# Gated linear attention: level and diagonal products as 32- and 64-wide squares, one to a column group of the array

## The reference, cut to what matters

```python
def _gla_chunkwise(q, k, v, lf, S):
    ...
        b = jnp.cumsum(lfc, axis=2)
        o = jnp.einsum('bhtk,bhkv->bhtv', qc * jnp.exp(b), S)
        pair = jnp.exp(jnp.where(tri, b[:, :, :, None, :] - b[:, :, None, :, :], -jnp.inf))
        a = jnp.einsum('bhtk,bhtsk->bhts', qc, pair * kc[:, :, None, :, :])
        o = o + jnp.einsum('bhts,bhsv->bhtv', a, vc)
```

## Time and profile before

| | |
|---|---|
| median of 3 runs | 4092.09 us (4091.87 to 4096.19) |
| the profiled execution's own time | 4100.84 us |
| its span | 4099.1 us |
| TensorE busy | 3935.4 us, 96% of the span |
| VectorE, ScalarE, GpSimd busy | 37%, 31%, 21% of the span |
| the attention stage that is changed | about 1590 to 2412 us of the span |

### The profile page before, as it was taken

How to read it: one execution, slowest core, us unless ns; L and a number is a source line. 1 busy time by engine, 2 the same in 40 slices (tenths; PEclk the granted TensorE clock), 3 DMA queues, 4 the chain that set the end, 5 groups by cost and what they waited for, 6 DMA issues and landing times.

```text
span 4099.1 us, 38980 instructions
## 1 busy us (share of the span) xinstructions
PE 3935.4 (96%) x15382; PEld 2318.2 (57%) x15382; DVE 1497.8 (37%) x2687; ACT 1257.4 (31%) x2313; POOL 862.4 (21%) x885
## 2 busy tenths in 40 slices
PE   7999999999999999999999999988999899999998
PEld 3555555655665546777777754435666644444443
DVE  2433332122221004777777731456666510010000
ACT  3444442222230023444444422764444300000000
POOL 0000000000100003666666630233434300000000
PEclk9999999999999999999999999999999999999999
DMA  5121012011002111100111021211001012222111
GB/s 203 44 88 44 29 30 89 1 62 62 1 31 103 57 61 62 38 34 35 40 42 42 27 75 51 77 63 42 20 38 39 24 46 80 90 77 73 65 71 49
DMA packets 23189, 225.74 MB, mean 55 GB/s; under 512 B 2528, under 2 KB 5088, under 8 KB 7520
## 3 DMA queue, kind: packets, MB, share of 16 engines
q1 hardware_dynamic: 23008, 223.25, 14.7%
HBM read 221.14 MB, written 2.10 MB: 54 GB/s over the span
## 4 chain that ended last, share of the span: by engine, by line
PE 91%; DVE 3%; ACT 2%; issue 2%; DMA 1%; POOL 1%; POOLq 0%; DVEq 0%; ACTq 0%; SPq 0%
PE bank L1088 8%; PE bank L1374 7%; PE bank L1035 6%; PE bank L1098 4%; PE bank L849 4%; PE bank L946 4%; PE bank L802 4%; PE bank L1385 4%; PE bank L1209 3%; PE bank L1007 3%; PE bank L1078 3%; PE bank L1350 3%; PE bank L788 3%; PE bank L1141 2%; PE bank L976 2%; PE bank L868 2%
## 5 line engine op out<-in xcount | busy, mean ns | idle before, releaser
L1088 PE MATMUL bank<-hT,ring 128*128 128x256 f32 (+1 forms) x1024 | 345.2, 486 | 0.0
L1374 PE MATMUL bank<-hT,ring 128*128 128x512 f32 x704 | 303.9, 595 | 2.4 <-DVE hT L1921 2.4
L1088 PEld LDWEIGHTS bank<-hT,ring 128*128 128x128 f32 x1024 | 189.9, 190 | 119.7 <-issue 108.1
L1035 PE MATMUL bank<-Y,ring 128*128 128x512 f32 (+1 forms) x704 | 249.2, 517 | 0.0
L1374 PEld LDWEIGHTS bank<-hT,ring 128*128 128x128 f32 x704 | 134.3, 191 | 172.0 <-issue 170.7
L1035 PEld LDWEIGHTS bank<-Y,ring 128*128 128x128 f32 x704 | 134.5, 191 | 114.7 <-issue 108.0
L1209 PE MATMUL bank<-hT,ring 128*128 128x512 f32 x384 | 181.7, 608 | 14.2 <-ACT arena L1758 8.8
L849 PE MATMUL bank<-hT,ring 128*128 128x256 f32 (+1 forms) x512 | 186.3, 500 | 2.4 <-ACT hT L1451 2.4
L802 PE MATMUL bank<-hT,ring 128*128 128x256 f32 (+1 forms) x512 | 182.3, 493 | 0.0
L1437 ACT ACTIVATE arena<-xT 128x512 f32<-128x512 f32 (+1 forms) x56 | 31.7, 568 | 484.3 <-PE bank L779 379.4
L1098 PE MATMUL bank<-ring,hT 128*128 128x128 f32 x1536 | 179.0, 275 | 0.0
(11 more groups left out here) (404 smaller groups left out, 6980.3 us busy)
## 6 DMA issues: line engine op xcount, KB each, us to landing
ring<-in_w SPq DMA_DIRECT2D x60, 2048.0 KB, 7.9
ring<-in_w SPq DMA_DIRECT2D x17, 1536.0 KB, 7.0
ring<-in_w SPq DMA_DIRECT2D x20, 1280.0 KB, 5.5
ring<-in_w SPq DMA_DIRECT2D x12, 1024.0 KB, 4.8
ring<-in_w SPq DMA_DIRECT2D x8, 1408.0 KB, 6.0
ring<-in_w SPq DMA_DIRECT2D x19, 512.0 KB, 3.6
xT<-in_xT SPq DMA_DIRECT2D x1, 3072.0 KB, 12.0
out<-arena SPq DMA_DIRECT2D x1, 2048.0 KB, 6.2
```

Source lines behind the costliest of these rows:

```text
L1035: ins = e.matmul(m[:, 0:b - a], w[:, k, sl(j % 2)], src[:, k, a:b], start=k == 0, stop=k == kt - 1)
L1088: ins = e.matmul(m[:, 0:b - a], w[:, k, sl(1 + d)], hT[:, k, a:b], start=k == 0, stop=k == 7)
L1374: ins = e.matmul(m, w[:, k, sl(2 * i + j % 2)], hT[:, k, 0:LAT], start=k == 0, stop=k == 7)
```

## The change

Each level's product, and the diagonal's, is computed only in the squares that can hold pairs of the level. `squares_of(m)` lists them. For m = 64 these are two squares of 64 x 64 in each chunk, the two off-diagonal ones. For every other level, and for the diagonal, they are four squares of 32 x 32: with m = 32 each key block of 32 against its neighbour's queries, below that each against its own. Each square is a matmul of its own, with 32 (or 64) stationary columns, 32 (or 64) moving columns and all 128 rows. It writes to the output partitions that its keys stand for, so that the four (two) squares of a chunk lie in four (two) different column groups of the array. What is left of the bank is not written; the masks let none of it through, and of the diagonal's bank it is written over later. The other engines' instructions stay as they are.

```diff
@@ -589,6 +589,16 @@
+        def squares_of(m):
+
+
+            n = 64 if m == 64 else 32
+            for c in range(NT):
+                for g in range(128 // n):
+                    r = g ^ 1 if m >= 32 else g
+                    yield (slice(128 * c + n * g, 128 * c + n * g + n), slice(128 * c + n * r, 128 * c + n * r + n),
+                           slice(n * g, n * g + n))
+
@@ -1128,8 +1138,8 @@
                 k = gl_QK[spot["gl_dqk", j]]
-                for c in range(NT):
-                    ins = e.matmul(m[:, sl(c)], k[:, sl(c)], gl_q_[j % 2][:, sl(c)], start=True, stop=True)
+                for kc, qc, p in squares_of(1):
+                    ins = e.matmul(m[p, qc], k[:, kc], gl_q_[j % 2][:, qc], start=True, stop=True)
                 ins.then_inc(up("gl_d_mm", j), 1)
@@ -1137,8 +1147,8 @@
                 x = gl_QK[spot["gl_qk", j, li]]
-                for c in range(NT):
-                    ins = e.matmul(m[:, sl(c)], x[:, 512 + 128 * c:640 + 128 * c], x[:, sl(c)], start=True, stop=True)
+                for kc, qc, p in squares_of(LEVELS[li]):
+                    ins = e.matmul(m[p, qc], x[:, 512:1024][:, kc], x[:, qc], start=True, stop=True)
                 ins.then_inc(up("gl_m_mm", (j, li)), 1)
```

## The result

| | before | changed |
|---|---|---|
| median of 4 runs each, side by side | 4093.44 us (4091.87 to 4096.19) | 4061.01 us (4059.42 to 4062.71) |
| ratio, 95% interval | | 0.992 (0.9903 to 0.9937) |
| profiled execution, its span | 4100.84, 4099.1 us | 4061.02, 4059.2 us |
| a head, from norm to norm | 52.24 us | 50.00 us |

The change makes the kernel faster by 0.8%: 32.4 us between the medians, 34 were forecast. Between the two profiled executions lie 39.8 us, but the one of before was slow for its kernel, 7.4 us above the median. The head tells more than either: it is 2.24 us shorter, and the forecast's sum of 36.0 us, shared among 16 heads, is 2.25 each. From the first head's diagonal to the first projection behind the last head the stage takes 814.82 us before (1599.00 to 2413.82) and 780.35 after (1598.04 to 2378.39): 34.5 us less.

A forecast was written before the change was run, and what follows sets the result against it. TensorE's unbroken row of matmuls bounds the kernel. 32-square groups save 34.7 us, 64-square groups 1.3, the last head gives back 1.6: net 34, so 4092.1 - 34 = 4058 us, range about 4047 to 4088.

The forecast's parts named there:

- the forecast's sum of 36.0 us: Saving over all heads: 34.7 us from 112 groups of 32-squares plus 1.3 us from 16 groups of 64-squares.
- The bound: In the stage's steady part TensorE's matmuls run unbroken, so a microsecond of matmul less is a microsecond of time less.
- A round, 0.030 us: Four 32-column records, one per column group, stream side by side in 30 ns; eight rounds make a group's 0.24 us.
- rival 1: Weights are not hidden inside a group of squares: 57 ns a round, about 9 us less, 4083 us; chance 0.11.
- The visit, 0.34 us: Cost of going from full-width matmuls into column groups and out: entry, first weights, emptying and exposed full-width weights, 0.34 us.
- The cover, 0.29 us a level: GpSimd needs 3.73 us a level, levels afterwards start 4.02 apart, so it keeps up by 0.29; waits cost nothing.
- rival 2: GpSimd or VectorE holds TensorE at four levels a head: 19 us given back, 4077 us; chance 0.10.
- The last head: TensorE waits for GpSimd before five of seven levels there, so 5 x 0.31 = 1.6 us are given back.
- Rivals 1 and 3: Rival 1 as above; the other: short squares don't overlap, 1.30 us a 32-square group, 4144 us, chance 0.11.
- Rival 4: Instructions between levels don't arrive fast enough, 56 ns each: 0.6 us more a level, 4169 us; chance 0.03.

The follow-up runs named there:

- e4: The changed kernel with the diagonal back in four full-width matmuls, only the levels in squares: 4068.39 us, ratio 0.993.
- e5: The kernel before, with one 32 x 32 square put ahead of each level's four full-width matmuls: 4141.87 us, ratio 1.011.
- e7: The kernel before, with four extra full-width matmuls of only 32 moving columns ahead of each level's four: 4192.33 us, ratio 1.0235.
- e6: The changed kernel with an extra set of squares, all into the first column group, ahead of each level's own: 4166.04 us, ratio 1.0166.
- e1: The changed kernel with its squares ordered by column group, all four chunks of one group before the next group: 4110.93 us, ratio 1.0037.
- e10: The changed kernel with squares ordered by column group two chunks at a time, four records of a group in a row: 4066.93 us, ratio 0.993.
- e11: The changed kernel with each level's whole set of squares computed twice, set after set, column groups alternating: 4101.47 us, ratio 1.0013.
- e8: The changed kernel with levels 32 and 16, 8 and 4, 2 and 1 paired, two levels in one visit: 4049.64 us, ratio 0.9886.

## Why the prediction was right

- **The bound.** TensorE's row of matmuls without a gap carried the gain one to one: 2.24 us a head less in the squares, 2.24 us a head less in the period. e4, e5 and e7 moved the head by 0.31, 2.62 and 6.25 us, as their groups' own changes add up.
- **A round, 0.030 us.** The rounds of four start 32 ns apart, not the 57 of rival 1. e6 has 31 ns a record within a group, and the change's eight rounds take 0.25 us where 0.24 stood. 64-squares: 0.61 us in the chain, 0.45 + 0.16 forecast.
- **The visit, 0.34 us.** From L761 and L916 (entry 0.09, first weights 0.03, emptying 0.11, full-width weights 0.11). The single starts of the change give 0.09, 0.02, 0.11 and 0.10, 0.33 in all. e5 measures 0.31 by itself, with a single square.
- **The cover, 0.29 us a level.** The forecast held, no wait in 735 us (rival 2), but this figure was not what covered it. 4.03 us is the distance of two levels only; in the same chain the last two of a head start 2.31 apart (1729.17 to 1731.48), less than GpSimd's 3.73. What counts is how long a product lies ready before its matmuls. By the trace of the second to the fourteenth head that is at least 1.41 us for GpSimd's before and 1.51 after, both at a head's first level, and 1.64 and 1.04 us for VectorE's, both at the fourth. The prediction allowed for 0.9 us of the first level's margin to go; it grew by 0.1, and the smallest one is now VectorE's.
- **The last head.** 1.6 us were to be given back, which leaves 0.65 of 2.25; it kept 0.86. Right in kind; the size came out near although the wait grew by 2.6 us, and what made up for it was not measured.
- **Rivals 1 and 3** were wrong for one reason: weights and squares of different column groups overlap. The Trainium skill (TensorE: Matmul & The Clock Gate, "The mechanism") has loads pulled ahead of running matmuls when their row group differs or when they go to a background weight buffer. Here all use all rows, and 32 loads take 0.35 us beside 32 matmuls, so the condition on the row group, on which rival 1 leaned, does not bind, as it did not in the earlier trace rows. Whether the buffer is the reason no run here shows.
- **Rival 4** was wrong where it was put: 56 ns an instruction was a rate that streaming set, and 32 pairs of load and matmul now start in 0.39 us. A trace of it may stand behind the 33rd record of a visit (0.05 us), which the change never reaches.

One premise of the text was too simple, at no cost here: it took the groups for streams that don't hold each other up. e1 and e6 show that this holds only while no more than three records wait for one group. The change lists the chunk outside and the group inside, which is the good order.

The stage's 34.5 us compares with the sum's 34.4 (36.0 less 1.6). The median's 32.4 us is uncertain by some 7 (its interval, 26 to 40 us). It does not contradict 34, and that the two lie so close says no more than that.

## What to carry to other kernels

A masked product that fills only small blocks can go to column groups if the array visits them seldom: price the visit first (0.3 us here, as much as three full-width 128-column records), put as many squares as possible into one visit, and write them so that neighbouring instructions go to different groups (with four records in a row to one group little was lost, with eight the whole gain). A visit's price shows partly on the neighbours' lines, so measure from a landmark of the stage (here norm to norm) and not by the changed line alone. Terms can be taken from another stage of the same trace if the form of the record is the same and only its length differs.

## What the runs showed of the hardware that was not expected

- Order within the squares: two, four and eight records in a row to one column group give 0.39, 0.42 and 0.83 us for the same 32 records (change, e10, e1). Matmuls of different column groups don't start strictly in program order: up to three records wait for their group while later ones go ahead (e6, e1).
- A full-width record with 32 moving columns costs 0.111 us, what one with 128 costs (e7); with 32 stationary columns it is 0.031 (e6).
- Of 64 records in one visit the second 32 cost 0.30 us, the first 0.25 (e11, e8); the cause is open.
- The Trainium skill (TensorEngine Tiling (Array Packing), "Key Properties") says that a change of the tiling mode drains TensorE. The trace agrees, and prices it here: about 0.31 us for a single 32 x 32 square among full-width matmuls (e5), of which 0.2 stand on the full-width neighbours.
